# First feed-forward matrix: two of the four sums of weight blocks made by accumulating transfers

## What is computed

```
gu = xn @ w_ffn_in[l]                       # (512, 1024) @ (1024, 2 * 2816)
g_ff, u_ff = gu[..., :D_FF_2], gu[..., D_FF_2:]
h = h + (jax.nn.silu(g_ff) * u_ff) @ w_ffn_out[l]
```

## Time and profile before

| | |
|---|---|
| median of 3 runs | 3265.59 us (3258.36 to 3269.38) |
| the profiled execution | 3251.48 us, its span 3249.7 us, mean granted TensorE clock 0.994 |
| busy, share of the span | PE 97%, PEld 88%, DVE 66%, ACT 47%, POOL 4% |
| DMA | 331.73 MB, mean 102 GB/s; 28.7% of 16 engines' time in the kernel's queue |
| loads of the units | 535 of 512.0 KB, median 3.7 us from issue to landing |
| loads into `fb` | 108 of 256.0 KB, median 2.5 us |

### The profile page before, as it was taken

How to read it: one execution, slowest core, us unless ns; L and a number is a source line. 1 busy time by engine, 2 the same in 40 slices (tenths; PEclk the granted TensorE clock), 3 DMA queues, 4 the chain that set the end, 5 groups by cost and what they waited for, 6 DMA issues and landing times. The chain is left out here.

```text
span 3249.7 us, 58922 instructions
## 1 busy us (share of the span) xinstructions
PE 3157.5 (97%) x24214; PEld 2863.2 (88%) x24214; DVE 2143.2 (66%) x3383; ACT 1535.2 (47%) x2651; POOL 137.5 (4%) x144
## 2 busy tenths in 40 slices
PE   9999999999999999999999988999999989999999
PEld 9998998999889988779998877879998867789997
DVE  7875544788577856448875766557874665667863
ACT  4553444355435543644553544444554444444553
POOL 0000111000000001000000100000000000000000
PEclk9999999999999999999999999999999999999999
DMA  4343222234323332112433221113332211123332
GB/s 180 143 141 110 95 72 90 76 136 148 117 88 127 134 121 93 53 66 88 143 134 123 86 72 60 37 63 117 131 142 97 99 66 53 41 83 119 141 126 72
DMA packets 104523, 331.73 MB, mean 102 GB/s; under 512 B 11264, under 2 KB 16640, under 8 KB 104256
## 3 DMA queue, kind: packets, MB, share of 16 engines
q1 hardware_dynamic: 104256, 327.96, 28.7%
HBM read 325.69 MB, written 2.23 MB: 101 GB/s over the span
## 5 line engine op out<-in xcount | busy, mean ns | idle before, releaser
L222 DVE TENSOR_TENSOR wlo<-raw,whi 128x1024 fp32r<-128x1024 f32 x319 | 387.7, 1224 | 433.3 <-ACT whi L214 432.6
L214 ACT ACTIVATE whi<-raw 128x1024 fp32r<-128x1024 f32 x319 | 334.2, 1055 | 386.4 <-PE ps L379 333.5
L803 PE MATMUL ps<-tz,whi 128*128 128x256 f32 x1728 | 477.6, 276 | 3.4 <-ACT tmp L975 3.4
L804 PE MATMUL ps<-tz,whi 128*128 128x256 f32 x1728 | 477.1, 276 | 0.0
L805 PE MATMUL ps<-tz,wlo 128*128 128x256 f32 x1728 | 477.1, 276 | 0.0
L241 PE MATMUL ps<-xh,whi 128*128 128x256 f32 x1424 | 410.3, 288 | 18.4 <-DVE wlo L222 11.1
L377 PE MATMUL ps<-whi,tz 128*128 128x512 f32 x1056 | 412.1, 390 | 0.0
L379 PE MATMUL ps<-whi,tz 128*128 128x512 f32 x1056 | 411.0, 389 | 0.0
L378 PE MATMUL ps<-wlo,tz 128*128 128x512 f32 x1056 | 410.9, 389 | 0.0
L243 PE MATMUL ps<-xh,wlo 128*128 128x256 f32 x1424 | 397.9, 279 | 0.0
L242 PE MATMUL ps<-xl,whi 128*128 128x256 f32 x1424 | 397.7, 279 | 0.0
(11 more groups left out here) (348 smaller groups left out, 6509.2 us busy)
## 6 DMA issues: line engine op xcount, KB each, us to landing
raw<-in_w SPq DMA_DIRECT2D x535, 512.0 KB, 3.7
fb<-in_w SPq DMA_DIRECT2D x108, 256.0 KB, 2.5
rows<-in_row SPq DMA_DIRECT2D x15, 512.0 KB, 4.6
xr<-in_xt SPq DMA_DIRECT2D x4, 512.0 KB, 6.6
xr<-in_x SPq DMA_DIRECT2D x1, 2048.0 KB, 7.4
mn<-bounds SPq DMA_DIRECT2D x8, 256.0 KB, 4.6
out<-tmp SPq DMA_DIRECT2D x4, 256.0 KB, 3.5
out<-rows SPq DMA_DIRECT2D x4, 256.0 KB, 2.3
```

The costliest lines, as they stand in the source:

```text
L214: a.activation(self.whi[u % NW][:, :], self.raw[u % NRAW][:, :], COPY).then_inc(*self.up("whi", u))
L222: v.tensor_tensor(self.wlo[u % NW][:, :], self.raw[u % NRAW][:, :], f32(self.whi[u % NW][:, :]), SUB).then_inc(*self.up("wlo", u))
L803: t.matmul(out, fh[:, sl], xh[:, k, :], start=first and k == 0, stop=False, skip_group_check=not first)
L804: t.matmul(out, fh[:, sl], xl[:, k, :], start=False, stop=False, skip_group_check=not first)
```

## The change

Sums 1 and 3 are no longer made by VectorE. Units w of the seven-product turns (`c.sums`) are loaded with their first half twice: the buffer holds [w1 | w1]. When that load has landed, GpSimd issues two transfers from memory that add to what lies in the buffer: w2 onto the first half (which gives sum 1) and g1, read from memory a second time, onto the second half (sum 3). Sum 2 is then the first half plus g1, sum 4 as before. ScalarE's and VectorE's parts for r = 1 become two instructions of 512 columns each, as their sources no longer lie side by side. The buffer of w is free only after low 3, which reads sum 3 in it. `es` shrinks from three blocks to one. GpSimd issues all 36 adds of a layer ahead of its norm steps.

```diff
-        s.dma_start(self.raw[u % NRAW][:, :], self.wst[u, :, :]).then_inc(*self.up(f"raw{u % NRAW}", u, by=16))
+        if u in self.sums:
+            s.dma_start(blocks(self.raw[u % NRAW][:, :], HK), over(self.wst[u, :, 0:HK], 2)).then_inc(*self.up(f"raw{u % NRAW}", u, by=16))
+        else:
+            s.dma_start(self.raw[u % NRAW][:, :], self.wst[u, :, :]).then_inc(*self.up(f"raw{u % NRAW}", u, by=16))
+
+    def add(self, g, u):
+
+        slot = f"{u % NRAW}"
+        g.wait_ge(*self.at("raw" + slot, u))
+        first, second = self.raw[u % NRAW][:, 0:HK], self.raw[u % NRAW][:, HK:2 * HK]
+        g.dma_start(first, self.wst[u, :, HK:2 * HK], accum_op=ADD).then_inc(*self.up("acc" + slot, u, by=16))
+        g.dma_start(second, self.wst[u - 1, :, 0:HK], accum_op=ADD).then_inc(*self.up("acc" + slot, u, by=16))
...
-                c.read[u0 + 2 * j + i] = "sum", s, j, 3 if i else 4
+                c.read[u0 + 2 * j + i] = ("flo", s, j, 3) if i else ("sum", s, j, 4)
+            c.sums.add(u0 + 2 * j + 1)
...
         elif r == 1:
             a.wait_ge(*c.at("sum", s, j, 2))
-            out, x = whi[:, :], self.es[:, 0:2, :].rearrange("p a n -> p (a n)")
+            a.activation(whi[:, 0:HK], self.raw(j, 1)[:, 0:HK], COPY)
+            out, x = whi[:, HK:2 * HK], self.es[:, :]
...
-            a.wait_ge(*c.at("sum", s, j, 3))
-            out, x = self.form(j, "S3")[0], self.es[:, 2, :]
+            a.wait_ge(*self.summed(j))
+            out, x = self.form(j, "S3")[0], self.raw(j, 1)[:, HK:2 * HK]
...
-        if n == 1:
+        if n == 2:
+            v.wait_ge(*self.summed(j))
             if j > FIRST7:
                 v.wait_ge(*c.at("flo", s, j - 1, 1))
-            v.wait_ge(*c.at(f"raw{(u + 1) % NRAW}", u + 1))
-            ins = v.tensor_tensor(s1, w1, w2, ADD)
-        elif n == 2:
-            v.wait_ge(*c.at("sum", s, j, 1))
-            if j > FIRST7:
                 v.wait_ge(*c.at("sum", s, j - 1, 4))
             v.wait_ge(*c.at(f"raw{u % NRAW}", u))
-            ins = v.tensor_tensor(s2, s1, g1, ADD)
-        elif n == 3:
-            if j > FIRST7:
-                v.wait_ge(*c.at("flo", s, j - 1, 3))
-            ins = v.tensor_tensor(s3, w1, g1, ADD)
+            ins = v.tensor_tensor(self.es[:, :], w[:, 0:HK], g[:, 0:HK], ADD)
...
     def gpsimd(self, g):
+        for j in range(FIRST7, KF):
+            self.c.add(g, self.u0 + 2 * j + 1)
         self.nm.gpsimd(g)
```

More of the change, by code:

```diff
@@ L191, in __init__ @@
         self.n_units = wst.shape[0]
-        self.freed, self.read = {}, {}
+        self.freed, self.read, self.sums = {}, {}, set()
     def begin(self):
@@ L791, in raw, with summed @@
         return self.c.raw[(self.u0 + 2 * j + i) % NRAW]
+    def summed(self, j):
+        u = self.u0 + 2 * j + 1
+        return self.c.at(f"acc{u % NRAW}", u)
     def fed(self, n):
@@ L992, in low_v @@
         elif r == 1:
-            hi, lo, x = hi[:, :], lo[:, :], self.es[:, 0:2, :].rearrange("p a n -> p (a n)")
+            v.tensor_tensor(lo[:, 0:HK], self.raw(j, 1)[:, 0:HK], f32(hi[:, 0:HK]), SUB)
+            hi, lo, x = hi[:, HK:2 * HK], lo[:, HK:2 * HK], self.es[:, :]
         elif r == 2:
@@ L996, in low_v @@
         else:
-            (hi, lo), x = self.form(j, "S3"), self.es[:, 2, :]
+            (hi, lo), x = self.form(j, "S3"), self.raw(j, 1)[:, HK:2 * HK]
         v.tensor_tensor(lo, x, f32(hi), SUB).then_inc(*c.up("flo", s, j, r))
@@ L1002, in sum_v @@
         c, s, u = self.c, self.s, self.u0 + 2 * j
-        (g1, g2), (w1, w2) = [[self.raw(j, i)[:, h * HK:h * HK + HK] for h in range(2)] for i in range(2)]
-        s1, s2, s3 = (self.es[:, i, :] for i in range(3))
-        if n == 1:
+        g, w = self.raw(j, 0), self.raw(j, 1)
+        if n == 2:
+            v.wait_ge(*self.summed(j))
             if j > FIRST7:
                 v.wait_ge(*c.at("flo", s, j - 1, 1))
-            v.wait_ge(*c.at(f"raw{(u + 1) % NRAW}", u + 1))
-            ins = v.tensor_tensor(s1, w1, w2, ADD)
-        elif n == 2:
-            v.wait_ge(*c.at("sum", s, j, 1))
-            if j > FIRST7:
                 v.wait_ge(*c.at("sum", s, j - 1, 4))
             v.wait_ge(*c.at(f"raw{u % NRAW}", u))
-            ins = v.tensor_tensor(s2, s1, g1, ADD)
-        elif n == 3:
-            if j > FIRST7:
-                v.wait_ge(*c.at("flo", s, j - 1, 3))
-            ins = v.tensor_tensor(s3, w1, g1, ADD)
+            ins = v.tensor_tensor(self.es[:, :], w[:, 0:HK], g[:, 0:HK], ADD)
         else:
@@ L1023, in sum_v @@
             v.wait_ge(*c.at("sum", s, j, 2))
-            ins = v.scalar_tensor_tensor(out=self.fb[:, 0:HK], in0=s2, scalar=-1.0, in1=g2, op0=MULT, op1=SUB)
+            ins = v.scalar_tensor_tensor(out=self.fb[:, 0:HK], in0=self.es[:, :], scalar=-1.0, in1=g[:, HK:2 * HK], op0=MULT, op1=SUB)
         ins.then_inc(*c.up("sum", s, j, n))
@@ L1092, in vector @@
         self.gate_v(v, 2)
-        for n in range(1, 4):
-            self.sum_v(v, FIRST7, n)
+        self.sum_v(v, FIRST7, 2)
         self.low_v(v, FIRST7, 0)
@@ L1102, in vector @@
                 self.low_v(v, j - 1, 2)
-            if not last:
-                self.sum_v(v, j + 1, 1)
             self.sum_v(v, j, 4)
@@ L1108, in vector @@
                 self.sum_v(v, j + 1, 2)
-                self.sum_v(v, j + 1, 3)
             if j > FIRST7:
@@ L2788, in build @@
             hf, tz = c.sb("hf", [P, KF, T], F32, scope), c.sb("tz", [P, 8 * 2 * T + LINE], F32R, scope)
-            es, fb = c.sb("es", [P, 3, HK], F32, scope), c.sb("fb", [P, 2 * HK], F32, scope)
+            es, fb = c.sb("es", [P, HK], F32, scope), c.sb("fb", [P, 2 * HK], F32, scope)
         start, stages, mixers = Start(c), [], []
```

## The result

The changed kernel takes 3358.31 us (median; the lowest run 3354.69), the kernel before 3264.36 us beside it (3258.36 to 3269.38): ratio 1.0285, 95% interval 1.0259 to 1.0311. It is 94 us slower. A fourth run of the changed kernel (5238.52 us, at a mean granted clock of 0.556) and one of the ten of `e3_aside` (8081.69 us) were slow executions, which count in the medians but in no ratio. The forecast of 3265 us (3254 to 3323) was wrong: the time lies above the range, and what happened is the first rival, the adds being late.

A forecast was written before the change was run, and what follows sets the result against it. The prediction took TensorE to bound the kernel, with VectorE's saved sums, the new chain and the extra DMA work each worth 0: 3249.7 + 0 + 0 - 0 for the span, 3265.6 + 0 = 3265 us for the median, range 3254 to 3323.

The forecast's parts named there:

- the first rival: At sum 2: adds later than 7.8 us after w's landing cost 48 us per us late, up to 3400 us; chance 0.18.
- TensorE bounds the loop, and VectorE's sums are worth nothing: Seven-product loop: TensorE busy 9.52 of 9.52 us; the 1.20 us taken off VectorE per turn become idle time, value 0.
- The split of low 1, the longer high 1, the later release: Per turn: VectorE 0.06 to 0.07 us more, ScalarE 0.2 more, w's load still out at 92.8; cost 0.
- The deadline: Path through w's buffer to sum 2: up to 11.9 us from w's issue, 7.8 from its landing, costs nothing turn after turn.
- The rival's sum: Late adds: each us over 7.8 delays 8 steps in each of six layers, 48 us in all; chance 0.18.
- The adds take 5.8 us from w's landing: Two GpSimd issues of 1.03 us each, then 3.7 us for the second add; bounds 2.9 and 10.6 us.
- The overlap on which I said it hung: Between a turn's two adds: the first lands under the second, as two 512 KB loads land within 4.1 us, not 7.4.
- The load of w lands in 4.1 us: Load of w beside g, issued at 92.8: landed at 96.9, where the adds start.
- More DMA work: Price 0: 512 KB of adds beside 1.25 MB of loads per turn: pair's loads already landed, only fb next, needed turns later; price 0.
- The mean share of 0.68: DMA share per turn, risen from 0.38, even if each added byte costs double.
- 2.0 us of cover: At sum 2: adds of 5.8 us against the 7.8 us that cost nothing turn after turn.
- GpSimd holding up VectorE: Rival: GpSimd's issues lengthen VectorE's gate and low 1, 20 us, or 165 for two whole operations; chance 0.05, at 3285 us.

The follow-up runs named there:

- e3_aside: Kernel before, all its sums on VectorE, plus the same GpSimd adds onto a block that nothing reads: 3263.07 us, ratio 1.002.
- e12_fb_w_g_first: Changed kernel with SyncE's load order fb, w, g, and sum 2 waiting for the first add alone, high 3 for the second: 3277.45 us, ratio 0.9993.
- e1_copies: Changed kernel with both adding transfers turned into plain copies of the same size, place and queue: 3259.94 us, ratio 1.0012.
- e7_release: Kernel before with only the later release of w's buffer, after low 3; sums on VectorE, no adds: 3254.35 us, ratio 1.0002.
- e5_apart: Changed kernel with SyncE issuing the next turn's loads only when the adds of the turn before have landed: 3524.51 us, ratio 1.0824.
- e4_one_add: Changed kernel with only sum 1 made by an adding transfer, sum 3 by VectorE in place: 3257.55 us, ratio 1.0011.
- e9_w_first: Changed kernel with SyncE's load order w, g, fb instead of fb, g, w: 3331.4 us, ratio 1.0236.
- e10_both: Changed kernel with load order w, g, fb, and sum 2 waiting for the first add alone, high 3 for the second: 3332.14 us, ratio 1.0238.
- e11_fb_w_g: Changed kernel with SyncE's load order fb, w, g instead of fb, g, w: 3299.27 us, ratio 1.0054.

## Why the prediction was wrong, by its own steps

- **TensorE bounds the loop, and VectorE's sums are worth nothing.** Right. `e12_fb_w_g_first` has VectorE at 2034.5 us instead of 2143.2 and no new wait, and gains nothing.
- **The split of low 1, the longer high 1, the later release.** Right: price 0. `e1_copies` contains all three and is at 1.0012, `e7_release` the release alone.
- **The deadline: 11.9 us from the issue of w to sum 2, turn after turn.** Right, as far as the table can tell. The rival's sum also holds: as each path spans two turns, half of the excess, 151 / 2 = 76 us, should reach TensorE; its stops grew by 68. What it left out is the lower clock behind the longer stops, up to some 19 us.
- **The adds take 5.8 us from w's landing.** A little short, and near only because two errors cancel. From the issue of the first to sum 2 it is 0.54 + 6.2 = 6.7 us in the mean (6.0 in `e5_apart`, with no load under way). GpSimd issues them 0.54 us apart and not 1.03, but the second lands after 6.0, not 3.7. The overlap on which I said it hung was there only in part: from the first issue to the second landing 0.54 + 6.0 = 6.5 us pass, against 7.4 for two of 3.7 one after the other. The Trainium skill's fit (DMA: Bandwidth & Descriptors, section Anatomy of one DMA), 2.6 us, is near the first copy of a pair here (2.9 in `e1_copies`) and short for each add (3.7 and 6.0). Its page Collectives: The Full Stack (section The bandwidth ceiling) says of the adding step of a collective that it pays with a second source read; the queue rows of this case agree in direction, 1.65 against 0.77 us of all engines.
- **The load of w lands in 4.1 us, and "More DMA work: Price 0".** This is the step that failed. I let the adds start when the loads had landed and said that next comes only `fb`. But with the adds 6 us long, those of j + 1 still run when `fb`, g and w of j + 2 go out, and w's load lands after 6.2 us in the median; to the issue of the first add it is 6.6 us in the mean (7.2 less 0.54). Of the 13.4 - 9.9 = 3.5 us by which the path is longer than forecast, 2.5 is the load and 0.9 the adds. The mean share of 0.68 that I worked out was right (0.70 in 120 to 180 us) and answered the wrong question: in the window from 90 to 92 us it is 1.03, all engines busy, just while w's load is in flight.

The load's 2.5 us have more than one source. The 4.1 of the earlier trace rows was too low from the start, as it is the median of g and w together. For these two loads (L229, issued at 92.8 and 93.2) the trace of before has

```profile
DMA to landing us min/median/max: 3.7/4.1/4.5
```

and w, the second, is the one with 4.5; over the loops of before it is 4.7 in the median. In the changed kernel the three loads of a turn go out closer together (1.33 us from `fb` to w instead of 1.58). With that form of the loop w lands after 5.1 to 5.3 us where there is no add beside it (`e5_apart`), one add (`e4_one_add`) or two copies (`e1_copies`), and after 6.2 with both adds. So of the 2.1 us between 4.1 and 6.2 about 1 goes with the second add, 0.6 is the misreading, and the 0.5 between belong to the new form of the loop; they aren't split further. How far w's place in the queue counts is shown by `e9_w_first` and `e10_both`: ahead of g and `fb` it lands after 4.5 us with both adds in the loop.

- **The margin.** I took 2.0 us of cover as enough against an unmeasured duration whose bounds I had put 7.7 us apart, and gave 0.18 to the late adds. With a path of several unpriced pieces on an engine group that they share, that chance was too low; and the range ended at 3323 although the upper bound gave 3400.
- **GpSimd holding up VectorE.** Refuted. GpSimd's issues take 0.86 and 1.22 us, and VectorE's operations are as long as before (L1016 1.22 and 0.68 to 0.69, L1028 0.69). The rule cited from the Trainium skill (SBUF — State Buffer, section Who interferes with whom) agrees.
- **What stays open.** Why the second add of a pair takes 6.0 us in the changed kernel and the first 3.7 isn't split up: part is the first add beside it (in `e5_apart`, with no load under way, 5.4 against 3.7), part the loads behind. Also open are the 12 us or more of TensorE's busy time that neither the clock nor the stops give.

## What to carry to other kernels

Work taken off an engine that already waits is worth nothing, while the thing that replaces it may stand on a path that matters: compare the new path (release of the buffer, load, adds, first reader) with the turns that the buffers allow, and price each transfer as it runs beside the others of that turn, not alone and not by a mean DMA share. An add by transfer costs the DMA engines about twice a copy; give it one more buffer, a wait of its own for each consumer, and put the load that has the longest way to go ahead of those that can wait. When an order is changed to help one transfer, look at who waits for the one that has become last.

## What was not expected of the hardware

- An adding transfer of 256 KB took 1.65 us of all 16 engines' time, a copy 0.77; GpSimd's issue of the second add took 1.22 us, of a copy 0.54.
- The transfers slow each other strongly: `fb`'s 256 KB landed after 2.5 us before, 3.1 beside copies, 4.7 beside adds, 5.5 when issued last.
- After a stop of 3.02 us TensorE ran about 3 us at the lower clock level, with 11 matmuls in 2 us instead of 18; over the loops the lower level stood for 37.5 us, worth up to some 19 us (an estimate) on top of 68 us of stops. In `e9_w_first`, `e10_both` and `e11_fb_w_g`, with no stop over 1.6 us, it did not come in the loops.
